# Expert results written to token order by an indirect scatter, and read back by plain loads

## What is computed

```
g_top   = argmax over 4 groups of (x @ w_rg + b_rg)
top 2 of the 8 experts in that group; weights = p_group * softmax(two logits)
for each chosen expert e: y = (silu(x @ w_gate[e]) * (x @ w_up[e])) @ w_down[e]
out[token] = sum over its two choices of weight * y
```

## Time and profile before

| what | value |
|---|---|
| median of 3 runs | 1827.53 us |
| the profiled execution | 1825.31 us, of which the span is 1823.3 us |
| TensorE matmuls busy | 1603.8 us (88%) |
| VectorE, ScalarE, GpSimd busy | 612.4, 366.4, 42.0 us |
| read from and written to device memory | 457.62 MB and 23.33 MB |
| expert stage of layer 0, first to last eviction of a result | 287.93 to 745.30 us |
| expert stage of layer 1, the same | 1300.55 to 1773.70 us |

### The profile page before, as it was taken

The page is one execution under the profiler, slowest core; times in us unless marked ns, Lnnn a source line. Parts: engine busy times, 40 slices in busy tenths (PEclk is TensorE's granted clock), DMA queues, the critical chain, the costliest instruction groups (busy, mean ns, idle before and its releaser), DMA issues. The chain is left out here.

```text
span 1823.3 us, 17766 instructions
## 1 busy us (share of the span) xinstructions
PE 1603.8 (88%) x6700; PEld 756.6 (41%) x6700; DVE 612.4 (34%) x1607; ACT 366.4 (20%) x779; POOL 42.0 (2%) x44
## 2 busy tenths in 40 slices
PE   7999969999989999499987788897999998998980
PEld 4444544444433333244447444444444443333330
DVE  2121343122121212333535799834322121212124
ACT  2000121111111111120001788812111111111111
POOL 0000110000000000100000000001000000000001
PEclk9999979999999999799996899998999999999995
DMA  5281139999999999641113000042999999999974
GB/s 185 69 316 75 62 147 406 420 422 421 421 421 420 421 421 420 258 120 46 42 51 139 1 1 1 1 154 92 369 421 421 421 421 421 421 421 420 422 321 152
DMA packets 116247, 482.36 MB, mean 265 GB/s; under 512 B 23600, under 2 KB 50224, under 8 KB 66224
## 3 DMA queue, kind: packets, MB, share of 16 engines
q1 hardware_dynamic: 103440, 455.55, 61.9%
q10 hardware_dynamic: 10400, 17.05, 2.5%
q0 software_dynamic: 2304, 8.39, 1.2%
HBM read 457.62 MB, written 23.33 MB: 264 GB/s over the span
## 5 line engine op out<-in xcount | busy, mean ns | idle before, releaser
L794 PE MATMUL ps<-raw,e_xT 128*64 128x512 f32 x2080 | 466.2, 594 | 46.3 <-DMA raw<-in_expert_w_up 46.3
L794 PEld LDWEIGHTS ps<-raw,e_xT 128*64 128x64 f32 x2080 | 156.2, 137 | 347.0 <-issue 346.4
L874 DVE TENSOR_TENSOR e_hid<-e_sg,ps 64x512 f32<-64x512 f32 x65 | 44.2, 679 | 636.7 <-ACT e_sg L841 636.7
L818 PE MATMUL ps<-raw,e_hT 128*64 128x512 f32 x1040 | 237.5, 598 | 0.0
L404 PE MATMUL ps<-c_hT,raw 128*128 128x512 f32 x384 | 165.0, 592 | 0.2 <-ACT c_hT L347 0.2
L841 ACT ACTIVATE e_sg<-ps 64x512 f32<-64x512 f32 x65 | 38.6, 594 | 466.7 <-PE ps L794 466.7
L768 PE MATMUL ps<-m_xhi,e_pick 128*128 128x512 f32 x276 | 118.8, 430 | 9.6 <-DVE e_pick L856 9.6
L818 PEld LDWEIGHTS ps<-raw,e_hT 128*64 128x64 f32 x1040 | 68.9, 136 | 122.3 <-issue 111.4
L1266 PE MATMUL ps<-a_spare,raw 128*128 128x512 f32 x256 | 111.8, 593 | 1.5 <-ACT a_spare L1118 1.5
L768 PE MATMUL ps<-m_xlo,e_pick 128*128 128x512 f32 x276 | 111.7, 405 | 0.0
L404 PEld LDWEIGHTS ps<-c_hT,raw 128*128 128x128 f32 x384 | 72.9, 190 | 91.7 <-issue 91.4
(11 more groups left out here) (228 smaller groups left out, 1447.2 us busy)
## 6 DMA issues: line engine op xcount, KB each, us to landing
raw<-in_expert_w_gate SPq DMA_DIRECT2D x130, 1024.0 KB, 27.3
raw<-in_expert_w_up SPq DMA_DIRECT2D x130, 1024.0 KB, 27.3
raw<-in_expert_w_down SPq DMA_DIRECT2D x130, 1024.0 KB, 27.6
slots_y<-e_ysb ACTq DMA_DIRECT2D x130, 128.0 KB, 6.7
raw<-in_conv_w_in SPq DMA_DIRECT2D x12, 1024.0 KB, 10.2
raw<-in_w_kv SPq DMA_DIRECT2D x6, 1024.0 KB, 12.5
raw<-in_conv_w_out SPq DMA_DIRECT2D x1, 4096.0 KB, 18.9
slots_y<-c_zero SPq DMA_DIRECT2D x16, 256.0 KB, 13.1
```

Of the source, the lines that this page charges most:

```text
L794: mm = pe.matmul(ps_gu[C - C * i:2 * C - C * i, :], xT[:, q % 2, k, u * C:(u + 1) * C], ring(m, L, p)[:, kk * F:(kk + 1) * F], start=(k == ...
L818: mm = pe.matmul(ps_y[c % 2][n * C:(n + 1) * C, :], hT[:, 2 * h + kk, :], ring(m, L, p)[:, kk * D + n * 512:kk * D + (n + 1) * 512], start ...
L874: dve.tensor_tensor(hid[:], sg[:], ps_gu[0:C, :], ALU.mult).then_inc(s_hid, 1)
```

## The change

Results are written to a table in token order, `pairs_y`, one for each layer, with row 2 x token + choice. So the row of each place has to be known where the result lies. TensorE gets it from the same 0/1 matrix: four more matmuls per pair of chunks multiply pick with two columns, 2 x token + 1 and the token's first slot within the pair. The first comes out as 0 for a place without a token; the second, compared with the place's number, tells which choice it is. VectorE makes row numbers of them (`dve_dest`, five small operations a pair), with 4096 added for an empty place, which puts it beyond the table. GpSimd issues one indirect DMA for each chunk, with a bounds check that leaves out such rows. The result is evicted as two halves of 64 partitions, so that a place's 1024 values stand in one partition; ScalarE issues no more stores. The table needs no zeros, so the 16 blank writes and the waits for them go. Combine loads the rows of 128 tokens, both choices, with one plain DMA of 1 MB for each tile, four in all, from SyncE's queue, ahead of the other loads of that stage. GpSimd now walks the list of conditional chunks too.

```diff
@@ setup
+            pool.iota(m.part[:], [[1, 1]], base=0, channel_multiplier=1, ...).then_inc(filled, 1)
+        @block.vector
+        def _(dve):
+            dve.wait_ge(filled, 4)
+            for i in range(2 * NT):
+                c = dve.tensor_scalar(m.code[:, i // NT, i % NT, 0:1], m.part[:], 2.0, float(2 * P * (i % NT) + 1),
+                                      ALU.mult, ALU.add)
+            c.then_inc(m.coded, 1)
+            dve.wait_ge(m.coded, 1)
@@ Combine
-                pool.indirect_dma_start(out=m.rows_y[:, t, k, :], out_offset=None, in_=m.slots_y[:, :],
-                                        in_offset=bass.IndirectOffsetOnAxis(ap=m.idx[:, t, k:k + 1], axis=0)
-                                        ).then_inc(self.come[2 * t + k], 16)
+    def loads(self, sp):
+        rows = m.pairs_y[self.L].rearrange("(t p k) d -> t p (k d)", p=P, k=2)
+        for t in range(NT):
+            sp.dma_start(m.rows_y[:, t].rearrange("p k d -> p (k d)"), rows[t]).then_inc(self.come[t], 16)
@@ conv_mixer, SyncE
-            sp.wait_ge(s_zero, 1)
-            blank = [m.slots_y[i * P:(i + 1) * P, :] for i in range(E * C // P, ROWS // P)]
-            for rows in blank:
-                for h in range(2):
-                    sp.dma_start(rows[:, h * S:(h + 1) * S], zero[:]).then_inc(s_blank, 16)
...
-            sp.wait_ge(s_blank, 32 * len(blank))
@@ experts, pe_gather
+            if h:
+                wait(pe, s_code, q + 1)
+                wait(pe, s_row, 2 * q)
+                for t in range(NT):
+                    mm = pe.matmul(ps_d, pick[:, q % 2, t, :], m.code[:, q % 2, t, :], start=(t == 0), stop=(t == NT - 1))
+                mm.then_inc(s_dest, 1)
@@ experts, act_step
-            wait(act, s_st[c % 2], c // 2 * 32)
-            act.activation(ysb[:, c % 2, :], ps_y[c % 2][:], ACT.Copy).then_inc(s_yev, 1)
-            act.wait_ge(s_yev, c + 1)
+            wait(act, s_st[c % 2], c // 2 * 16)
             for n in range(2):
-                act.dma_start(m.slots_y[c * C:(c + 1) * C, n * 512:(n + 1) * 512], ysb[n * C:(n + 1) * C, c % 2, :]
-                              ).then_inc(s_st[c % 2], 16)
+                y = act.activation(ysb[:, c % 2, n * 512:(n + 1) * 512], ps_y[c % 2][n * C:(n + 1) * C, :], ACT.Copy)
+            y.then_inc(s_yev, 1)
+        def pool_step(pool, c):
+            wait(pool, s_row, c + 1)
+            wait(pool, s_yev, c + 1)
+            pool.indirect_dma_start(out=m.pairs_y[L][:, :], in_=ysb[:, c % 2, :], in_offset=None,
+                                    out_offset=bass.IndirectOffsetOnAxis(ap=m.to_row[:, c:c + 1], axis=0),
+                                    bounds_check=2 * S - 1, oob_is_err=False).then_inc(s_st[c % 2], 16)
@@ experts, VectorE
+            dve.tensor_scalar(m.code[:, g % 2, :, 1], m.slot[:, :, 0], -1.0, float(GS), ALU.max, ALU.min).then_inc(s_code, 1)
+        def dve_dest(dve, own, g):
+            dve.wait_ge(s_dest, g + 1)
+            token, choice = ps_d[:, 0:1], ps_d[:, 1:2]
+            own.step(dve.tensor_scalar(dest[:, 0:1], choice, m.part[:], None, ALU.not_equal))
+            own.step(dve.tensor_tensor(dest[:, 0:1], dest[:, 0:1], token, ALU.add))
+            own.step(dve.tensor_scalar(dest[:, 1:2], token, 0.0, FAR, ALU.is_equal, ALU.mult))
+            for u in range(PAIR):
+                half = slice(u * C, (u + 1) * C)
+                dve.scalar_tensor_tensor(out=m.to_row[:, PAIR * g + u:PAIR * g + u + 1], in0=dest[half, 0:1], scalar=-1.0,
+                                         in1=dest[half, 1:2], op0=ALU.add, op1=ALU.add).then_inc(s_row, 1)
@@ experts, GpSimd
-            pool.wait_ge(r.s_table, 1)
-            n = pool.value_load(m.novf[0:1, 0:1], min_val=0, max_val=N_OVF)
+            n = chunks(pool, lambda c: pool_step(pool, c))
@@ final_norm
+            arrived.loads(sp)
             sp.dma_start(gb[:], m.a["norm_final"]...).then_inc(s_gb, 16)
-            arrived.gathers(pool)
```

More of the change, by code:

```diff
@@ L47 @@
 N_OVF = 2 * S // C
-ROWS = (E + N_OVF) * C
+FAR = 4096.0
 NPIECE = 6
@@ L102, in program @@
         m.rstd = sb("rstd", [P, 5, NT])
-        m.idx = sb("idx", [P, NT, 2], U32)
+        m.code = sb("code", [P, 2, NT, 2], F32R)
+        m.part = sb("part", [P, 1])
+        m.to_row = sb("to_row", [C, E + N_OVF + PAIR], U32)
         m.wts = sb("wts", [P, NT, 2])
@@ L107, in program @@
         m.ps = [ctx.enter_context(nc.psum_tensor(f"ps{i}", [P, 512], F32)) for i in range(8)]
-        m.slots_y = nc.dram_tensor("slots_y", (ROWS, D), F32, kind="Internal").ap()
+        m.pairs_y = [nc.dram_tensor(f"pairs_y{L}", (2 * S, D), F32, kind="Internal").ap() for L in range(2)]
         m.ready = sem("constants_ready")
@@ L185, in _ @@
                       allow_small_or_imprecise_dtypes=True).then_inc(filled, 1)
-            pool.wait_ge(filled, 3)
+            pool.iota(m.part[:], [[1, 1]], base=0, channel_multiplier=1,
+                      allow_small_or_imprecise_dtypes=True).then_inc(filled, 1)
+            pool.wait_ge(filled, 4)
             pool.affine_select(out=m.ident[:], in_=m.ident[:], compare_op=ALU.not_equal, fill=1.0, base=0,
@@ L190, in _ @@
                                pattern=[[1, P]], channel_multiplier=-1).then_inc(filled, 1)
-            pool.wait_ge(filled, 5)
+            pool.wait_ge(filled, 6)
             pool.tensor_copy(m.identb[:], m.ident[:]).then_inc(m.ready, 1)
             pool.wait_ge(m.ready, 1)
+        @block.vector
[6 more added lines that the diff above has]
+            dve.wait_ge(m.coded, 1)
 class Norm:
@@ L256, in __init__ @@
         self.own, self.added = m.sem(f"k{L}_own"), m.sem(f"k{L}_added")
-        self.come = [m.sem(f"k{L}_in{i}") for i in range(2 * NT)]
-    def gathers(self, pool):
+        self.come = [m.sem(f"k{L}_in{i}") for i in range(NT)]
+    def loads(self, sp):
         m = self.m
+        rows = m.pairs_y[self.L].rearrange("(t p k) d -> t p (k d)", p=P, k=2)
         for t in range(NT):
-            for k in range(2):
-                pool.indirect_dma_start(out=m.rows_y[:, t, k, :], out_offset=None, in_=m.slots_y[:, :],
-                                        in_offset=bass.IndirectOffsetOnAxis(ap=m.idx[:, t, k:k + 1], axis=0)
-                                        ).then_inc(self.come[2 * t + k], 16)
+            sp.dma_start(m.rows_y[:, t].rearrange("p k d -> p (k d)"), rows[t]).then_inc(self.come[t], 16)
     def vector_add(self, dve, t, k):
         m = self.m
-        dve.wait_ge(self.come[2 * t + k], 16)
+        dve.wait_ge(self.come[t], 16)
         if k:
@@ L689, in slots @@
             own.step(c)
-            own.step(dve.tensor_reduce(m.slot[:].rearrange("p t k -> p k t"), self.oh, AX.X, ALU.add))
-            dve.tensor_copy(m.idx[:], m.slot[:]).then_inc(self.s_slots, 1)
+            dve.tensor_reduce(m.slot[:].rearrange("p t k -> p k t"), self.oh, AX.X, ALU.add).then_inc(self.s_slots, 1)
             dve.wait_ge(self.s_slots, 1)
@@ L880, in dve_step @@
                 dve_pick(dve, own, c // PAIR + 2)
+            else:
+                dve_dest(dve, own, c // PAIR + 1)
         def chunks(eng, step):
@@ L917, in _ @@
         def _(pool):
-            pool.wait_ge(r.s_table, 1)
-            n = pool.value_load(m.novf[0:1, 0:1], min_val=0, max_val=N_OVF)
+            n = chunks(pool, lambda c: pool_step(pool, c))
             for half in s_st:
-                pool.wait_ge(half, E // 2 * 32)
+                pool.wait_ge(half, E // 2 * 16)
             with pool.If(0 < n):
-                pool.wait_ge(s_st[0], (n + (E + 1) >> 1) * 32)
-                pool.wait_ge(s_st[1], (n + E >> 1) * 32)
+                pool.wait_ge(s_st[0], (n + (E + 1) >> 1) * 16)
+                pool.wait_ge(s_st[1], (n + E >> 1) * 16)
         @block.vector
@@ L933, in _ @@
             r.vector_tail(dve)
+            dve_dest(dve, own, 0)
             chunks(dve, lambda c: dve_step(dve, own, c))
```

26 lines of the change are left out of this document (14 added, 12 removed).

## The result

The changed kernel takes 1805.37 us at the median of four runs (1803.95 to 1807.29), the kernel before 1826.95 beside it. The ratio is 0.9882 with a 95% interval from 0.9865 to 0.9900, so it is faster by 21.6 us. The profiled execution took 1805.73 us with a span of 1804.0; the span is 19.3 us shorter. The prediction was 1807.

What follows compares the result with a forecast made beforehand. The DMA engines' bytes were taken to bound the expert stages. Terms -18 + 1 - 4 + 0.4 + 0 + 0.4 = -20.2 brought the profiled 1825.31 us to 1805.1; with 2.2 for the median, 1807, range 1801 to 1812 (chance 0.40).

Steps and rivals of the forecast that it cites:

- rows left out: Expert stages: 8.65 MB fewer result bytes shorten DMA time; -18 us, between 15 and 24, if remaining rows are spread evenly.
- end of layer 0: After layer 0's last result: second half eviction and the scatter's landing delay the next stage; +1 us (0.9 to 1.9).
- reading back, layer 0: Plain loads of both choices let layer 0's adds finish earlier; -4 us, bounds -4 and +4.
- end of layer 1: Conditional chunks after layer 1: GpSimd's ladder adds 0, TensorE's bodies grow some 3%; +0.4 us.
- last stage: Adds some 2 us earlier, but the gain vector's load behind 4.2 MB takes it back; 0 (-2 to +1).
- start, to the first gather of layer 0: Setup gains one GpSimd operation and eight on VectorE; +0.4 us (0.2 to 0.9).
- The added work of TensorE, VectorE, ScalarE and GpSimd: Expert stages: hidden because DMA is the bound; TensorE's matmuls 0.37 to 0.56 us a chunk, otherwise costing 24 to 36 us.
- between: Rival for the scatter's sharing over engines: shares partly even, half of the gain, 1812 to 1820 us; chance 0.13.
- sign of being wrong: Late pace of evictions in the expert stages, 15.58 us before: the forecast is wrong if it doesn't fall below 15.45.
- Fixed shares: Rival: scatter gives each engine four consecutive places, so first engines save nothing; 1824 us, with a loss 1821 to 1832; chance 0.33.
- Nothing skipped: Rival: the scatter moves empty places somewhere all the same, ending at 1824 us; chance 0.04.
- Eight rows an engine: Rival: scatter keeps blocks of eight rows an engine, slower; about 1868 us, or about 1840 with two blocks of four; chance 0.10.

Runs made afterwards that it cites:

- experiment 4: Changed kernel with nothing skipped: empty places written to spare rows of a longer pairs_y, all 64 rows a chunk going out; 1822.06 us, ratio 0.9970.
- experiment 2: Changed kernel with novf's 32 bytes allocated behind raw2, so raw2 starts at 84448, 224 above a multiple of 256 as before the change; 1816.46 us, ratio 0.9944.
- experiment 1: Kernel before with 288 unused bytes of SBUF ahead of raw2, so it starts at 84480 and not 84192; 1817.32 us, ratio 0.9947.
- 7: Changed kernel reading its rows back by eight indirect gathers of GpSimd in place of four plain loads; 1809.32 us, ratio 0.9906.
- experiment 10: Changed kernel with the final gain vector's load between the second and third of the four plain loads, not behind them; 1804.05 us, ratio 0.9872.
- experiment 5: Changed kernel with ranks reordered so that four consecutive ranks stand on one DMA engine, same rows and bytes; 1819.74 us, ratio 0.9963.
- 8: Changed kernel with the sixteen conditions on overflow chunks nested in one another, not one after the other; 1792.08 us, ratio 0.9807.
- 9: Kernel before with the sixteen conditions on overflow chunks nested in one another; 1810.00 us, ratio 0.9920.
- 11: Changed kernel with SyncE issuing each layer's four plain loads inside the expert stage once the last scatter landed, not behind the barrier; 1797.60 us, ratio 0.9843.

## Why the prediction was right, and where only by balance

| step | predicted | measured | by |
|---|---|---|---|
| rows left out | -18 | -14.9 (stages), -16.7 (medians) | 4 |
| the same, `raw2` at its old address | -18 | -12.3 (stages) | 2 against before |
| address of `raw2`, kernel before | not seen | -10.4 (stages), -9.0 (medians) | 1 |
| the same, changed kernel | not seen | -12.1 (stages), -11.1 (medians) | 2 |
| end of layer 0 | +1 | +3.3 | trace |
| reading back, layer 0 | -4 | -4.1 (SyncE's first DMA to the projections); -3.95 | trace; 7 |
| end of layer 1 | +0.4 | +2.9 | trace |
| last stage | 0 | +1.1 | trace |
| start, to the first gather of layer 0 | +0.4 | -0.3 | trace |
| between these rows | 0 | +2.1 | trace |

The stages are 24.4 us shorter, which is the sum of 12.3 and 12.1, and of 14.9 and 10.4 but for 0.9 us. With the rows of the ends, the reading back and the start, the trace gives -19.4, and the span shrank by 19.3. The last row is 1.2 us in the first pair of chunks of layer 0 and 0.9 in the attention stage with the first pair behind it. The trace of experiment 10, the same code up to there, has its first eviction at 287.98 and not at 288.85, so these 2.1 us are not put down to the change.

**Scattered rows.** The mechanism is shown: what the DMA engines carry, the fullest one above all, sets the length of the stages, and the rows left out are spread closely enough to even. The term was mis-sized: 12.3 to 16.7 for 18. The half row a chunk that was put on the fullest engine, 160 rows over both layers, was too little for this sharing, in which engine e carries the places 2e, 2e+1, 32+2e and 33+2e. The packet records bear out the pairs: the last scatter of the changed kernel, 21 rows with nothing beside it, moved in two waves of 11 and 10 packets of 4 KB, where four consecutive rows on an engine make four waves. The second pair rests on experiment 5: four consecutive places an engine would have left the fullest engine at 128 and 132 rows in both orders, yet its order took 14.4 us longer. With ranks filled from 0 up, the first engine still carries 86 and 94 rows, 180 of 260, by the 4 KB packets of each scatter (experiments 4 and 5 were reckoned with 92 for layer 1); 80 x 159 ns is 12.7 us, where the mean, 128 rows, would have given 21. Why experiment 4 gave 2 to 4 us more than that is open.

**What failed: the address.** The prediction counted bytes and took the rate of 421 GB/s as given. It was not: the rate hung on where `raw2` begins, and a diff that adds small tiles ahead of it moves it. Experiments 1 and 2 turn this on and off, in both kernels, at 5 to 7 us a layer. The Trainium skill has a rule near it, on the page "DMA: Bandwidth & Descriptors", section "How a descriptor splits into AXI transactions": a descriptor that doesn't start at a multiple of 256 bytes costs additional beats. The runs agree for `raw2`, 224 bytes above such a multiple, with 313 against 309 ns for 8 KB; they don't show the beats. They don't agree for `raw`: by the rule its six pieces, 128 above a multiple, would pay too, but in the changed kernel 96 to 99% of all 8 KB packets within the stages took 309 ns, those pieces included. So the address is shown as the cause, and which boundary counts is not; no run moved `raw2` to a third offset. The sum of allocations was there to be made before the prediction.

**The small terms.** Reading back was right. The end of layer 0 was not: up to the landing it cost only 0.3 us and not 1 (last eviction to landing at 738.2, 4.6 us; the old one was 4.3), but behind it GpSimd's drain of 2.77 us wasn't in the sum. Its price on the path is borne out by 8 and 9 (3.4 us with the scatter) and 11 (SyncE starts 3.8 us earlier when it doesn't wait for it). In layer 1 TensorE's branches cover the drain; the 2.9 us there are TensorE's own, whose branches went from 294 to 1508 ns at the median. Why is open: its conditional bodies grew by four matmuls in every second one, far less than the branches did, and no run changed these bodies alone. The gain vector was indeed what the first scaling waited for (2.8 us). The added work of TensorE, VectorE, ScalarE and GpSimd was hidden as said where the DMA set the pace: the late pace of evictions fell, to 15.18 by the last pair of layer 0 (718.42 to 733.60). In the early part, where TensorE sets it, the pace went from 13.85 to 13.95 us in the mean, 0.1 us a chunk for the 0.37 to 0.56 that were estimated.

**The balance.** The forecast had the rows left out 1 to 6 us too good, the ends and the last stage 5.9 too good, the start 0.7 too bad; the address, 9 to 12, was missing. Without it the changed kernel takes 1816.5 (experiment 2), 9.5 us off the forecast, outside its 1801 to 1812 and where the rival "between" stood. The prediction was near because two errors met. Its own sign of being wrong wouldn't have told: a late pace below 15.45 us is what experiment 1 shows (15.33) with every row still written.

**The rivals.** Fixed shares of four consecutive rows lose by 5: that layout takes 1819.7, with the address's gain in it, and isn't what the scatter does. Nothing skipped takes 1822, and is out by the queue's 8.40 MB. Eight rows an engine is out with the sharing above.

## What to carry to other kernels

Where the DMA engines bound a stage, compare their rate at a full share in both kernels before counting bytes, and look at the SBUF address of every large buffer after an edit that adds small tiles ahead of it: 288 unused bytes were worth 9 us here, over a third of the change. Count the rows of the fullest engine, not the mean. And look for what follows the last transfer: a drain, a row of branches or a barrier can hide a step or be laid bare by it, and loads that need only data, not the barrier, can be issued ahead of it.

## What the runs showed that was not expected

- A place left out of an indirect scatter still costs a packet of 4 bytes and 9 ns.
- A 64-row scatter gives each DMA engine two pairs of rows, 32 places apart, not four consecutive ones (the first pair by the packet records, the second by experiment 5).
- The address of a weight buffer, 224 bytes above a multiple of 256, cost 313 ns a packet of 8 KB for 309, and 128 bytes above one cost nothing.
- GpSimd's drain took 2.76 to 2.78 us in a stage where it had issued scatters, 41 ns in one where it had not, though the last scatter had landed.
- With the list of sixteen conditions, fifteen of them not met, SyncE's first DMA behind layer 1 came 20.0 and 22.9 us after the last eviction; nested, it came 4.7 and 8.1 us after it. TensorE's sequencer took 294 and 1508 ns a branch at the median, where ScalarE and GpSimd passed theirs at 45 ns. Nested, the kernel is 13 to 17 us faster.
